# Output projection of the second block's mixing stage in split float32r form

## The reference, cut to what matters

```python
def second_block(x, p, ...):
    ...
    y = jax.nn.sigmoid(ma) * ya + jax.nn.sigmoid(mb) * yb
    h = layer_norm_2(DEEPNORM_ALPHA * h + y @ w_out[i], ln1_g[i], ln1_b[i])
    m = moe(h, w_router[i], b_router[i], w_up[i], b_up[i], w_down[i], b_down[i])
    h = layer_norm_2(DEEPNORM_ALPHA * h + m, ln2_g[i], ln2_b[i])
    h = h + jax.nn.sigmoid(h @ w_ple_gate[i] + b_ple_gate[i]) * (p[i] @ w_ple[i])
    return h
```

## Time and profile before

| | |
|---|---|
| median of 3 runs | 2415.95 us (2414.32 to 2416.76) |
| profiled execution, own time | 2414.09 us |
| its span, first to last instruction | 2412.3 us |
| mean granted TensorE clock | 0.999 of full speed |
| TensorE busy | 2350.4 us (97%) |
| VectorE, ScalarE busy | 1167.5 us (48%), 806.8 us (33%) |
| read from HBM | 662.63 MB, 275 GB/s over the span |

### The profile page before, as it was taken

One profiled execution on the slowest core, in us unless ns is written; L12 is line 12 of the kernel. 1 busy time (PEld: TensorE's weight loads), 2 busy tenths in 40 slices (PEclk: granted clock), 3 DMA queues, 4 the chain that ended last, 5 costly groups with the idle time before them and its releaser, 6 DMA issues.

```text
span 2412.3 us, 33169 instructions
## 1 busy us (share of the span) xinstructions
PE 2350.4 (97%) x13423; PEld 1603.9 (66%) x13423; DVE 1167.5 (48%) x1603; ACT 806.8 (33%) x1011; POOL 195.2 (8%) x90
## 2 busy tenths in 40 slices
PE   8999999999999999999999999999999999999999
PEld 7889989888888998888898974333333333333334
DVE  5567866755756776675686753111211111111114
ACT  4454344544444434444448322111111111111111
POOL 0002502200200250220020000000000000000000
PEclk9999999999999999999999999999999999999999
DMA  7665453556556545456546589999999999999994
GB/s 250 210 203 172 158 183 129 191 187 200 176 191 209 163 153 192 138 177 201 183 142 195 165 340 366 426 428 426 429 428 427 427 427 428 428 426 428 428 419 181
DMA packets 221163, 665.25 MB, mean 276 GB/s; under 512 B 9905, under 2 KB 164527, under 8 KB 191104
## 3 DMA queue, kind: packets, MB, share of 16 engines
q1 hardware_dynamic: 221056, 663.71, 72.6%
HBM read 662.63 MB, written 1.05 MB: 275 GB/s over the span
## 4 chain that ended last, share of the span: by engine, by line
PE 79%; DMA 16%; DVE 2%; ACT 2%; issue 1%; SPq 0%; DVEq 0%
PE ps L711 19%; PE ps L722 14%; PE ps L696 11%; DMA ring<-in_w_up_dram 11%; PE ps L1324 10%; PE ps L1368 6%; DMA work<-in_w_up_dram 5%; PE ps L807 5%; PE ps L1294 2%; PE ps L1285 2%; PE ps L1346 1%; PE ps L1467 1%; PE ps L1159 1%; PE ps L917 1%; PE ps L970 1%
## 5 line engine op out<-in xcount | busy, mean ns | idle before, releaser
L2077 DVE TENSOR_TENSOR ring_halves<-ring,ring_halves 128x2048 fp32r<-128x2048 f32 x206 | 509.3, 2480 | 206.5 <-ACT ring_halves L1550 206.2
L711 PE MATMUL ps<-x_halves,ring_halves 128*128 128x512 f32 (+1 forms) x2560 | 457.2, 339 | 0.0
L1550 ACT CAST ring_halves<-ring 128x2048 fp32r<-128x2048 f32 x206 | 393.0, 1908 | 125.2 <-PE ps L722 101.0
L711 PEld LDWEIGHTS ps<-x_halves,ring_halves 128*128 128x128 f32 x2560 | 394.5, 189 | 59.2
L2612 DVE TENSOR_SCALAR work<-work 128x128 f32<-128x128 f32 x64 | 19.3, 344 | 683.0 <-PE ps L1324 683.0
L1324 PE MATMUL ps<-ring,work 128*64 128x512 f32 x1376 | 306.1, 594 | 24.2 <-DMA ring<-in_w_up_dram 23.5
L722 PE MATMUL ps<-ring_halves,work_halves 128*128 128x512 f32 x1184 | 288.9, 391 | 0.2
L722 PEld LDWEIGHTS ps<-ring_halves,work_halves 128*128 128x128 f32 x1184 | 221.6, 188 | 47.1 <-issue 2.3
L696 PE MATMUL ps<-x_halves,ring_halves 128*128 128x256 f32 x2016 | 250.4, 285 | 0.7 <-ACT work L1844 0.7
L1324 PEld LDWEIGHTS ps<-ring,work 128*64 128x64 f32 x1376 | 96.9, 137 | 226.8 <-issue 176.7
L696 PEld LDWEIGHTS ps<-x_halves,ring_halves 128*128 128x128 f32 x2016 | 244.2, 192 | 2.9 <-ACT work L1844 1.2
(11 more groups left out here) (280 smaller groups left out, 2173.0 us busy)
## 6 DMA issues: line engine op xcount, KB each, us to landing
ring<-in_w_up_dram SPq DMA_DIRECT2D x86, 2048.0 KB, 35.5
work<-in_w_up_dram SPq DMA_DIRECT2D x42, 2048.0 KB, 36.9
ring<-in_w_down_dram SPq DMA_DIRECT2D x42, 2048.0 KB, 39.8
ring<-in_w_in_dram SPq DMA_DIRECT2D x52, 1024.0 KB, 5.3
ring<-in_ffn_gate_dram SPq DMA_DIRECT2D x44, 1024.0 KB, 5.3
ring<-in_ffn_up_dram SPq DMA_DIRECT2D x44, 1024.0 KB, 5.4
ring<-in_ffn_down_dram SPq DMA_DIRECT2D x44, 1024.0 KB, 4.9
work<-in_w_down_dram SPq DMA_DIRECT2D x21, 2048.0 KB, 40.2
```

Of the source, the lines that this page charges most:

```text
L711: mm = pe.matmul(out, wt[:, o:o + P], x, start=(k == 0 and n == 0), stop=(k == DT - 1 and n == 1))
L1550: nc.scalar.copy(high_of(name)[:], ring[:, s, :]).then_inc(hi_done.add(name), 1)
L2077: v.tensor_tensor(ring_halves[s][:], ring[:, s, :], high_of(name)[:].bitcast(F32), ALU.subtract)\
```

## The change

The output projection runs in split form. ScalarE rounds the four parts of `w_out` (`weight_high`) and of y (`rounded`), VectorE subtracts (`weight_low`, `rounded_off`), and TensorE sums three one-pass products for each of the float32 ones. The weights' high halves lie in cell 11 (parts 0 and 3, one after the other) and in the two spare cells (parts 1 and 2, `OUT_HIGH`); y's halves lie in scratch. TensorE's blocks come in another order, so that each part's weights are given back earlier. As the spare cells are in use, HEAD's down weights 2 and 3 are loaded behind the parts' release, after HEAD's other weights. Cells 10 and 11 move back in CELLS, from the third pair to the seventh, and wait for `w2o3`.

```diff
--- before.py
+++ after.py
@@ -65,7 +65,8 @@
 BDOWN, BUPROWS, ROUTER, BEFORE = 5120, TH + 1024, 20000, 20256
 EXTRA = (XC, R, 1024, Y, V, IG)
 SPARE = RING + len(EXTRA)
-CELLS = (6, 7, 8, 9, 10, 11, 0, 1, 12, 13, 2, 3, 4, 5, 14, 15, 16, 17)
+CELLS = (6, 7, 8, 9, 0, 1, 12, 13, 2, 3, 4, 5, 10, 11, 14, 15, 16, 17)
+OUT_HIGH = (ML, SPARE, SPARE + 1, ML)
 TURN = len(CELLS) // 6
 TURNS = (EXPERTS - 2) // TURN
 HEAD, LAST = 0, TURN + 1
@@ -218,18 +219,20 @@
-        with nc.sbuf_tensor("ring", [P, RING, SLOT], F32) as ring, nc.sbuf_tensor("work", [P, WORK], F32) as work:
+        with nc.sbuf_tensor("ring", [P, RING, SLOT], F32) as ring, nc.sbuf_tensor("work", [P, WORK], F32) as work, \
+                nc.sbuf_tensor("spare", [P, 2, SLOT], F32) as spare:
             pass
         ring_halves = [sb(f"ring_halves{i}", [P, SLOT], F32R) for i in range(XH)]
         x_halves = sb("x_halves", [P, 2 * SLOT], F32R)
         ring_halves += [None, None, sb("ring_halves11", [P, SLOT], F32R)]
         work_halves, at = {}, 0
-        for off, size in ((HDH, 1536), (HDL, 1536), (MEMH, 2048)):
+        for off, size in ((HDH, 1536), (HDL, 1536), (Y, 2048), (MEMH, 2048)):
             if off > at:
                 sb(f"between{off}", [P, off - at])
             work_halves[off] = sb(f"work_halves{off}", [P, size], F32R)
             at = off + size
         sb("after_halves", [P, WORK - at])
+        spare_halves = [sb(f"spare_halves{i}", [P, SLOT], F32R) for i in range(2)]
         h = sb("h", [P, TT, D])
         hn = sb("hn", [P, TT, D])
         hT = sb("hT", [P, DT, T])
@@ -252,7 +255,6 @@
         smax = sb("smax", [P, HEADS, TT])
         ssum = sb("ssum", [P, HEADS, TT])
         brout = sb("brout", [1, 32])
-        spare = sb("spare", [P, 2, SLOT])
         ps = ctx.enter_context(nc.psum_tensor("ps", [P, 8, 512], F32))
@@ -303,6 +305,20 @@
         mh = work_halves[MEMH][:].rearrange("p (k t) -> p k t", k=DT)
         ml = ring_halves[ML][:].rearrange("p (k t) -> p k t", k=DT)
+        def out_high(j):
+            s = OUT_HIGH[j]
+            return ring_halves[s] if s < RING else spare_halves[s - SPARE]
+        def y_high(j):
+            tile, at = (work_halves[HDL], 512 * j) if j < 3 else (work_halves[HDH], K)
+            return tile[:, at:at + 512].rearrange("p (k t) -> p k t", k=2)
+        def y_low(j):
+            return work_halves[Y][:, 512 * j:512 * j + 512].rearrange("p (k t) -> p k t", k=2)
         def hidden_high(c):
             return work_halves[HDH][:, 512 * (c % 3):512 * (c % 3) + 512]
@@ -416,6 +432,8 @@
                     slot_of[x] = i
                     sp.wait_ge(used[i].sem, used[i].at(x))
                     plain(sp)
+                if s2 == ML:
+                    slot_used(sp, "w2o3")
                 if s < RING:
                     sp.dma_start(ring[:, s:s + 2, :].rearrange("p s n -> p (s n)"), src).then_inc(loaded[s].sem, 16)
                     return
@@ -438,6 +456,8 @@
                 for x, i in ((name, SPARE), (second, SPARE + 1)):
                     used[i].add(x)
                     slot_of[x] = i
+                for j in (1, 2):
+                    slot_used(sp, f"w2o{j}")
                 sp.dma_start(spare[:], src.rearrange("p (s n) -> p s n", s=2)).then_inc(loaded[SPARE].sem, 16)
             def columns(wt, c0):
@@ -612,8 +632,6 @@
                          a["p_2"].rearrange("l a (t p) n -> p (l a t) n", p=P)).then_inc(ple_in.add("ptok"), 16)
             sp.dma_start(w(V, 2048, "p (k n) -> p k n", k=2), rows(a["w_ple_2"].rearrange("a k n -> (a k) n"), 0))\
                 .then_inc(ple_in.add("wple"), 16)
-            load_spare(weight(HEAD, "d", 2), weight(HEAD, "d", 3), wdn[:, 0, 1, :])
-
             def expert_up(i, e):
                 for k in range(0, DT, 2):
                     load_pair(weight(i, "u", k), weight(i, "u", k + 1), wup[:, e, k // 2, :])
@@ -630,6 +648,7 @@
             slot_used(sp, "ma3")
             expert_up(HEAD, 0)
             expert_down(HEAD, 0, (0,))
+            load_spare(weight(HEAD, "d", 2), weight(HEAD, "d", 3), wdn[:, 0, 1, :])
             sp.dma_start(work[0:32, BDOWN:BDOWN + 1024], a["b_down_2"].rearrange("a e n -> (a e) n"))\
                 .then_inc(bias_in.add("bdown"), 16)
             with counted(book, sp, "e", TURNS, loaded + used) as e:
@@ -1153,46 +1172,42 @@
             by_columns("ma2", 0)
             by_columns("ma3", 1)
-            def w2o_part(j, kk, t, halves_of=(0, 1)):
-                s = slot_of[f"w2o{j}"]
+            after = ("A",)
+            def w2o_part(j, t, halves_of=(0, 1)):
+                high, low = out_high(j), ring_halves[slot_of[f"w2o{j}"]]
+                tok = slice(t * P, t * P + P)
                 for half in halves_of:
-                    mm = pe.matmul(ps[:, acc_bank(after, t) + half, :], yT[:, 2 * j + kk, t * P:t * P + P],
-                                   ring[:, s, kk * D + half * 512:kk * D + half * 512 + 512],
-                                   start=(j == 0 and kk == 0), stop=(j == 3 and kk == 1))
+                    for kk in range(2):
+                        o = kk * D + half * 512
+                        x_high, x_low = y_high(j)[:, kk, tok], y_low(j)[:, kk, tok]
+                        for n, (x, wt) in enumerate(((x_high, high), (x_low, high), (x_high, low))):
+                            mm = pe.matmul(ps[:, acc_bank(after, t) + half, :], x, wt[:, o:o + 512],
+                                           start=(j == 0 and kk == 0 and n == 0), stop=(j == 3 and kk == 1 and n == 2))
                 return mm
             def y_part(j):
-                arrived(f"w2o{j}")
-                pe.wait_ge(dve_done.sem, dve_done.at(("y", "g", j)))
-
-            after = ("A",)
+                pe.wait_ge(dve_done.sem, dve_done.at(("out low", j)))
+                pe.wait_ge(dve_done.sem, dve_done.at(("y low", j)))
             y_part(0)
             for t in range(TT):
                 open_bank(acc_bank(after, t), "w2o")
                 open_bank(acc_bank(after, t) + 1, "w2o")
-                for kk in range(2):
-                    mm = w2o_part(0, kk, t)
+                mm = w2o_part(0, t)
             release(mm, "w2o0")
-            def w2o_last(t):
-                for half in range(2):
-                    for kk in range(2):
-                        mm = w2o_part(3, kk, t, (half,))
-                    if half == 0:
-                        full(mm, ("half", after, t))
-                return mm
-
-            for j in (1, 2):
-                y_part(j)
-                for kk in range(2):
-                    w2o_part(j, kk, 0)
+            y_part(1)
+            w2o_part(1, 0)
+            y_part(2)
+            w2o_part(2, 0)
+            release(w2o_part(1, 1), "w2o1")
             y_part(3)
-            full(w2o_last(0), ("t0", after))
-            for j in (1, 2):
-                for kk in range(2):
-                    mm = w2o_part(j, kk, 1)
-                release(mm, f"w2o{j}")
+            full(w2o_part(3, 0, (0,)), ("half", after, 0))
+            full(w2o_part(3, 0, (1,)), ("t0", after))
+            release(w2o_part(2, 1), "w2o2")
+            full(w2o_part(3, 1, (0,)), ("half", after, 1))
             transposes(after, 0, hn)
-            release(w2o_last(1), "w2o3")
+            release(w2o_part(3, 1, (1,)), "w2o3")
             def router(t):
@@ -1924,11 +1939,31 @@
             squares("g", 8)
             through_r("ga", 3, ACT.Gelu_apprx_tanh)
             roots([("ms", "g", j) for j in range(2)], 256, 0, 6)
+            def weight_high(j):
+                s = slot_of[f"w2o{j}"]
+                if j == 3:
+                    slot_used(act, "w2o0")
+                act.wait_ge(loaded[s].sem, loaded[s].at(f"w2o{j}"))
+                done(nc.scalar.copy(out_high(j)[:], ring[:, s, :]), ("out high", j))
+            def rounded(j):
+                act.wait_ge(dve_done.sem, dve_done.at(("y", "g", j)))
+                done(nc.scalar.copy(y_high(j), yT[:, 2 * j:2 * j + 2, :]), ("y high", j))
+            weight_high(0)
             through_r("ma", 0, ACT.Sigmoid)
+            weight_high(1)
             through_r("ma", 1, ACT.Sigmoid)
+            weight_high(2)
             through_r("ma", 2, ACT.Sigmoid)
+            rounded(0)
+            rounded(1)
             through_r("ma", 3, ACT.Sigmoid)
             root_table()
+            rounded(2)
+            weight_high(3)
+            rounded(3)
             ln(("A",), ("ln1_g_2", "ln1_b_2"), 0, turned_p)
@@ -2506,13 +2541,18 @@
             def inverse(j):
                 bank_empty(6 + j, ("ms", "g", j))
                 link(v.reciprocal(work[:, Q + 512 * j:Q + 512 * j + 512], work[:, Q + 512 * j:Q + 512 * j + 512]))
-            inverse(0)
-            next_low("ma0")
-            inverse(1)
-            for j in range(2):
-                mine(("ga", j))
-                times("ma", j)
-            for j in range(4):
+            def weight_low(j):
+                s = slot_of[f"w2o{j}"]
```

(26 more changed lines are left out.)

## The result

The changed kernel takes 2418.19 us as a median of 20 runs (2415.32 to 2420.49), the kernel before, on the same chips, 2415.68 us (2412.87 to 2417.23). The ratio is 1.0013, with a 95% interval of 1.0007 to 1.0019: 2.5 us longer by the medians, within what was called no change, and in the other direction than the forecast of -0.85 us. (In the series of the experiments one execution of bank, one of fill and two of the kernel before beside them took 2730 to 8356 us; no ratio counts these.) The profiled execution took 2416.91 us, span 2415.1, mean granted clock 0.998.

A forecast was written before the change was run, and what follows sets the result against it. TensorE bounds the experts until 1785 us, then the weight transfer stream. Product savings of 5.65 us, less a 4.45 us stand and 0.35 us given back, made -0.85 us: 2415.1 us as a median, range 2411.5 to 2419.

The forecast's parts named there:

- rival 1: TensorE's clock falls to half speed in its 4.5 us stand in the projection: +0.8 us, 2416.8; chance 0.33.
- -5.65 + 4.45 + 0.35 = -0.85 us, to the end: Whole kernel: products saved, plus TensorE's stand for bank 5, plus late gain given back before the experts.
- 1455 to 1460 with TensorE busy 4.00 us of 5 at clock 1.00: Window before the experts in the old profile, cited as evidence against the clock falling during the stand.
- if twice as long, +2.4: Within rival 1, projection: half clock lasting twice 3.3 us would make the forecast sum +2.4 us.
- 96 one-pass products at 0.227 us, -5.65: TensorE, projection: split products take 21.8 us where the float32 form took 27.5.
- Bank 5 is late, TensorE stands 4.5 us: Projection, second block: VectorE's inserted subtractions delay mixed(3), freeing bank 5 at 1419.1; the first block ends at 1414.7.
- The clock stays: Projection: the forecast kept TensorE at full clock through the stand, with no clock term in its sum.
- The transposes 0.8 us later: After the projection's tokens 0: transposes start 0.8 us later than 1436.12, with 1.4 us of products behind.
- Late gain of 0.35 given back: Between transposes and experts: copies of the transposed block hold TensorE, leaving 0.85 us gain, not 1.3.
- Moved transfers free: Transfer queue before the experts: 4.9 us of moved loads go into idle time; the tail's loads cost nothing.
- ScalarE's roundings hidden: Projection: ScalarE's high pieces are ready before needed, the last part with 3 us to spare.
- The change is worth what that pair moves: Weight stream: the end moves with the pair issued at 1490.7, set by TensorE's arrival; its end moves 1497.0 to 1496.1.

The follow-up runs named there:

- bank: Changed kernel with VectorE's mixed(3) moved ahead of rounded_off(1), weight_low(2) and rounded_off(2), so bank 5 is freed earlier; 2411.44 us, ratio 0.9986.
- fill: Changed kernel with sixteen extra, unused products put into TensorE's pause between first and second projection block; 2414.75 us, ratio 0.9998.
- experiment 1: Kernel before, float32 projection kept, with only the moved transfers (new CELLS order, later spare load); 2414.57 us, ratio 1.0000.
- again_d: Changed kernel, nothing altered, one further profiled execution; 2419.67 or 2419.78 us (the text gives the two times of this pair together).
- early: Changed kernel with mixed(3) earlier, p's transposes behind the first projection block, first embedding block ahead of the router; 2408.75 us, ratio 0.9976.
- bank2: The bank kernel (changed kernel, mixed(3) earlier on VectorE) run again on another chip; 2411.66 us, ratio 0.9987.
- again_e: Changed kernel, nothing altered, another profiled execution beside again_d; 2419.67 or 2419.78 us (times given together).
- loads: Same run as experiment 1: kernel before with the moved transfers alone; 2414.57 us, ratio 1.0000.

## Why the prediction was wrong

**The step that failed** is the one at rival 1: the forecast carried "-5.65 + 4.45 + 0.35 = -0.85 us, to the end" with no term for the clock, and gave the falling clock a chance of 0.33. It fell in all six profiled executions of the changed kernel, near the end of the pause, and took 1.5 to 1.7 us behind it in four and 2.9 to 3.1 in two. The evidence that I set against it, 1455 to 1460 with TensorE busy 4.00 us of 5 at clock 1.00, holds idle time cut into several short pauses; a single one of 3.9 us was in no row. The rule that I cited from the Trainium skill, page "TensorE: Matmul & The Clock Gate", section "Why this matters for your kernels" (no longer idle gaps between bursts of matmuls), agrees with the runs at this pause: 3.9 us gave a low stretch each time, 3.47 us in the one profile with it, and 0.5 us gave none behind it. The time of rival 1, 2416.8, is what the executions of the shorter kind show (2414.7 to 2416.9). Its "if twice as long, +2.4" covers the longer kind's stretch behind the pause, not the second one in the layer norm, which I had nowhere.

Point by point:

- *96 one-pass products at 0.227 us, -5.65.* Right: 0.231 us at full clock, 0.4 us less gain.
- *Bank 5 is late, TensorE stands 4.5 us.* Right in place, engine and instruction; 3.91 us measured (some 4.0 with the pipelined end of the last product). The bank was free at 1418.76 when the 2.06 us of the opening are taken off, forecast 1419.1.
- *The clock stays.* Wrong: +1.5 us (1.5 to 1.7 in four profiles), in the longer kind 2.9 to 3.1 and another 1.7 in the layer norm.
- *The transposes 0.8 us later.* 1440.42 less 2.06 is 1438.36, against 1436.12: 2.2 later, which is the 0.8, the clock's 1.5, the 0.4 of the products and the shorter pause (-0.5).
- *Late gain of 0.35 given back.* From there to the experts the forecast had 22.7 us (1436.9 to 1459.6); 22.73 measured. Right where the clock holds.
- *Moved transfers free.* Right, shown by experiment 1. The tail's rows and weights came out as forecast too: the spans grew by no more than the start of the experts.
- *ScalarE's roundings hidden.* Right: TensorE's only stand in the projection is that of bank 5.
- *"The change is worth what that pair moves".* Right: experts +2.72 us, span +2.8 (again_d: +5.57 and +5.5). In early and bank2, which start the experts 4.3 to 4.4 us earlier than before, 0.7 to 0.8 of that is lost again.

With the measured terms: -5.3 (products) + 4.0 (pause) + 0.35 + 1.5 (clock) = +0.55, where the stage shows +0.66. What made the result larger is the second kind of execution.

The time of 2418.19 lies inside the range that I gave, but that is no merit of the sum: the range was wide, and the longer kind of execution stood in none of my cases.

What is shown: that the low stretch at the pause comes from TensorE having no work (fill), and that the pause comes from bank 5 (bank). Only argued: which part of early's form keeps the clock up in the layer norm, the embedding block ahead of the 32-column router products or the missing transposes of p. Open: why the clock falls earlier in the same pause in some executions and then stays low twice as long, and the tail.

## What to carry to other kernels

When faster matmuls uncover a wait, price the wait with its clock: here 3.9 us of standing cost 5.4 us, and in two of six profiles 6.9 and another 1.7 in the next stage. Look first at what holds the wait, here three subtractions on VectorE ahead of the two instructions that free a PSUM bank, and put those two first; what can't be removed may be filled: 3.79 us of products kept the clock up here, 0.60 us of transposes in the same pause did not. And profile the same kernel more than once: the first four profiles here showed one low stretch at the pause, and by their times most executions had more.

## What the runs showed of the hardware

- In the very same pause of 3.91 us the clock fell to its 1.2 GHz level 0.1 to 0.5 us before TensorE restarted in four profiles and stayed there 3.41 us (1.5 to 1.7 us lost); in two it fell 0.7 and 1.0 us before the restart and stayed 6.83 us (2.9 and 3.1 lost).
- A low stretch also came in the layer norm where TensorE had stood for no more than 0.27 us (bank, fill), behind transposes and 32-column products, in some executions of a kernel and not in others (bank and bank2). In bank, fill, again_d and again_e the fall lay within 0.5 us of the start of the first embedding block.
- The opening's 64 products took 14.05 us in some executions and 15.7 to 16.3 in others, with the float32 projection (before, loads) and with the changed one, which moves everything behind by about 2 us. In the first profile after the change ten of them stood 0.43 us apart in place of 0.216, with the clock's column at 1.00: there the pace of the products tells more than the column. Two profiles are to be compared from a common instruction on.
